# Quarters of a projection moved between transposes and behind score products in a hybrid decoder layer

## The chip, the cores and the metric

The kernel runs on one core of a Trainium2 chip. The metric is the time of one execution on the device in microseconds; several executions are taken and their median is given. The profile is of one further execution. Engines are TensorE (PE in the rows), VectorE (DVE), ScalarE (ACT), GpSimd (POOL) and SyncE (SP), which here only issues transfers.

## The reference, cut to what matters

One decoder layer on 1024 tokens of width 1024, in float32. A combined input projection `u = x @ w_in` is split by columns among four causal mixers and their merge gates; the four results are projected, gated, summed and projected again, and a mixture of 64 experts follows.

```
u = x @ w_in
(conv_in, swa_q, swa_k, swa_v, ret_q, ret_k, ret_v, ret_g,
 nsa_q, nsa_kc, nsa_vc, nsa_ks, nsa_vs, nsa_kw, nsa_vw, nsa_gate, merge_gate) = jnp.split(u, ...)
y_conv = conformer_conv(conv_in, ...) @ p_conv
y_swa = banded_attention(swa_q, swa_k, swa_v, ..., window 128, sink) @ p_swa
y_ret = retention(ret_q, ret_k, ret_v, ret_g, ...) @ p_ret
y_nsa = native_sparse_attention(nsa_q, ...) @ p_nsa
merged = (gts[..., 0, :] * y_conv + gts[..., 1, :] * y_swa
          + gts[..., 2, :] * y_ret + gts[..., 3, :] * y_nsa)
x = layer_norm(ALPHA * x + merged @ w_out)
x = layer_norm(ALPHA * x + moe_ffn(x))
```

## The kernel before, in words

The kernel has two parts, `front` (the mixers) and `back` (output projection, experts). The change is in `front` alone, whose engines all walk one list of items, `SCHEDULE`, written out by the function `schedule`. Each engine takes from every item what is its own, in the order of the list; semaphores tie the engines together. So to move an item in the list moves it on TensorE, ScalarE, VectorE and GpSimd at once.

**The projection.** The columns of `w_in` are cut into 58 chunks of 128. A chunk has two halves of 512 tokens, and a half has two quarters of four of the eight contraction steps: quarter `q` belongs to chunk `q // 4`, half `q // 2 % 2`. A quarter is 12 matmuls of 128x512 (L620), since weights and x are each split into a high and a low part and three products are summed. The halves alternate between PSUM banks 0 and 1. When an odd quarter is done, ScalarE copies the half out (`half`); for the 32 chunks of merge gates this is a tanh into `gate_out` and a store of 256 KB to `gates` (L848, L850), which first waits until the store of two halves ago has landed. After each fourth quarter GpSimd splits the weights of the chunk two ahead (L558, L560), and SyncE then loads another (L469). Quarters are always issued in the order of their numbers, 232 in all; `adv(n)` puts the next n of them into the list, `upto(c)` all up to chunk c.

**Fills.** A `fill` is a group of up to eight transposes on TensorE into bank 6 and one copy out of it by ScalarE (L938, L924). All fills share this bank, and each waits for the copy of the one before:

```
B = bank[6]
if f:
    pe.wait_ge(fill_out, f)
```

There are four fills behind the normalisation of each of two pairs of retention heads (`ret_norm` on VectorE, which ends with `ret_fin`, L1118), two for `swa_v`, one for the gates of the sparse attention, two for `vsvw`, one for `pe`, eight behind the compressed scores, and in both attentions one to four per pair of heads, which carry the probabilities to the products with the values (`pv`, L812).

**Attention.** The function `attention` walks over pairs of heads and blocks. In slot k it issues the score product of pair k+1 (`score`, L790, banks 2 to 5), VectorE's maxima of it (`max`, which end in `m_neg`, L1145 and L1148), VectorE's norms of pair k (L1162, L1166), the fills of pair k-1 with ScalarE's exponentials of pair k+1 behind the last of them, and `rate` quarters, counted by a running debt over the fills. A score product waits for the maxima of all pairs before it (`pe.wait_ge(max_done, 2 * p)`), the fills of a pair for its norms. The sliding-window attention has 16 pairs and two quarters per pair. The sparse attention has 32, alternately `win` (up to 5 key blocks) and `sel` (up to 8), and what quarters are left, divided by 30.

**Order of the parts around the change.** Retention of pair 0, more chunks, retention of pair 1, the `swa_v` fills, sliding-window attention (quarters 121 to 152), fills for gate, vsvw and pe, nine quarters, hidden products of the compression (L745) with a quarter after each, compressed scores with three quarters each, sparse attention (quarters 196 to 231, the last one behind the first fill of its last but one slot).

**Behind the attention.** SyncE waits until all 232 quarters are done (`half_done`), since the loads that follow overwrite their operands: merge weights `p_raw` (L492), then eight pieces of the stored branch results `yt` (L503), the last of them only when the last attention tile is stored, and the gates (L498). ScalarE and VectorE split the pieces into high and low parts (L993, L1226). TensorE multiplies by the merge weights, eight column groups j of two halves (L833), and VectorE gates and sums them (L1237, L1240); from the second group on a half waits for the merge of the half before in the same banks.

Of the kernel before, what the change touches and what calls it, by code (L numbers as in the profile page):

```python
# [163 lines left out]
def schedule():  # L164

    items = [('xt', g) for g in range(8)] + [('mm', 0), ('mm', 1)] + [('xt', g) for g in range(8, 16)]
    state = dict(q=2, fill=0, pv=0)
    last = 4 * NCH  # L170

    def adv(n):
        for _ in range(n):
            if state['q'] < last:
                items.append(('mm', state['q']))
                state['q'] += 1

    def upto(c):
        adv(max(0, 4 * c - state['q']))

    def fill(kind, *a):
        items.append(('fill', state['fill'], kind, a))
        state['fill'] += 1

    upto(WHERE['ret_q', 0])
    items.append(('conv_h',))
    for k in range(CONV_K):
        items.append(('tap', k))
        adv(2 if k % 3 == 0 else 1)
    adv(2)  # L190
    for c in ('conv_mean', 'conv_var', 'conv_out'):
        items.append((c,))
        adv(4)

    def retention(p):
        items.append(('ret_a', p, 0))
        for n in range(NT):
            adv(1)
            if n + 1 < NT:
                items.append(('ret_a', p, n + 1))  # L200
            items.append(('ret_b', p, n))
        items.append(('ret_norm', p))
        adv(11)
        for g in range(4):
            fill('ret', p, g)
        items.append(('ret_store', p))
    upto(WHERE['ret_g', (0, 1)] + 1)
    retention(0)
    upto(WHERE['ret_g', (1, 1)] + 1)
    retention(1)  # L210
    upto(WHERE['swa_v', 0] + 1)
    for g in range(2):
        fill('swa_v', g)
        adv(1)

    def attention(pairs, rate):


        debt = 0.0
        waiting = []  # L220

        def product():

            pr, blocks = waiting.pop()
            items.append(('pv', state['pv'], pr['p'], blocks))
            pr['last_pv'] = state['pv']
            state['pv'] += 1
            if pr['c'] == 1 and pr['kind'] != 'win' and blocks[-1] == pr['nb'] - 1:
                items.append(('out', pr['kind'], pr['n']))

        def both(what, k):
            for e in range(2):
                items.append((what, 2 * pairs[k]['p'] + e))
        for k in range(-1, len(pairs) + 1):
            if k + 1 < len(pairs):
                pr = pairs[k + 1]
                if pr['kind'] == 'sel' and pr['c'] == 0:
                    items.append(('sel_table', pr['n']))
                items.append(('score', pr['p']))
                both('max', k + 1)  # L240
            if 0 <= k < len(pairs):
                both('norm', k)
            if k < 1 and k + 1 < len(pairs):
                both('exp', k + 1)
            if k >= 1:
                prev = pairs[k - 1]
                groups = [tuple(range(a, min(a + 2, prev['nb']))) for a in range(0, prev['nb'], 2)]
                prev['first_fill'] = state['fill']
                prev['last_fill'] = state['fill'] + len(groups) - 1
                for g, blocks in enumerate(groups):  # L250
                    fill('pair', prev['p'], blocks, state['pv'] + len(waiting))
                    if g == len(groups) - 1 and k + 1 < len(pairs):
                        both('exp', k + 1)
                    debt += rate / len(groups)
                    adv(int(debt))
                    debt -= int(debt)
                    if waiting:
                        product()
                    waiting.append((prev, blocks))
        product()  # L260
    attention(SWA, 2.0)
    upto(WHERE['gate', 0] + 1)
    fill('gate')
    for g in range(2):
        fill('vsvw', g)
    fill('pe')
    adv(9)
    for l in range(0, CMP_LEN, HID_STEP):
        items.append(('hidden', l))
        adv(1)  # L270
    items.append(('hidden_t',))
    adv(1)
    items.append(('compress',))
    adv(1)
    for n in range(NT):
        items.append(('cmp_score', n))
        adv(3)
        fill('cmp', n)
    attention(NSA, (last - state['q']) / (len(NSA) - 2))
    adv(last)  # L280
    return items


SCHEDULE = schedule()


# [2005 lines left out]
```

## Time and profile before

| | |
|---|---|
| time, three runs | 2136.57 us median (2134.29 to 2140.7) |
| the profiled execution | 2132.68 us; its span 2130.9 us |
| mean granted clock of TensorE | 0.985 |
| busy share of the span | TensorE 95%, VectorE 63%, ScalarE 40%, GpSimd 26% |
| first score, sliding window / sparse | 422.35 us / 693.92 us |
| last product with the values ends | 932.37 us |

Times in rows are microseconds from the span's start. In a timeline a row is one instruction or a run of equal ones: start, time busy, engine, source line, operation, output and inputs, count; in brackets the idle time of the engine before it and what ended that. The granted clock is a share of full speed (2.4 GHz); its lower level is 0.50 (1.2 GHz). Matmuls overlap in the pipeline, so their starts are compared, not their durations.

### The profile page before, as it was taken

How to read it: one execution, taken by the hardware profiler on the slowest of the kernel's cores; microseconds unless marked ns; L12 is line 12 of the kernel's file. 1: busy time of each engine (PE TensorE's matmuls, PEld its weight loads, DVE VectorE, ACT ScalarE, POOL GpSimd, SP SyncE). 2: the span in 40 equal slices, each digit the busy share in tenths (PEclk: the TensorE clock that was granted, in tenths of full speed). 3: DMA queues.
4: the chain of work that ended last, by engine and by line, in shares of the span. 5: the costliest groups of instructions: out<-in, count | busy, mean ns of one | idle time of the engine just before them, and what ended most of it. 6: DMA issues, size and time to landing. Idle time of an engine off the chain costs nothing.

```text
span 2130.9 us, 33125 instructions
## 1 busy us (share of the span) xinstructions
PE 2032.9 (95%) x9741; PEld 1443.2 (68%) x9742; DVE 1349.5 (63%) x2792; ACT 852.5 (40%) x1433; POOL 554.5 (26%) x358
## 2 busy tenths in 40 slices
PE   6999999899999999989999979999999999999995
PEld 5887777777778666658745537666666666666662
DVE  2594543444026677768646737777777777777756
ACT  2111221234111344440022336666666666666643
POOL 2343231323312211002110033322323333232324
PEclk8999999999999999999999999999999999999998
DMA  5123211222622111057580267899897989899857
GB/s 183 50 55 94 89 50 40 70 55 56 148 75 80 58 50 36 18 179 266 188 332 30 109 268 223 304 347 345 308 352 263 350 300 336 309 303 313 300 172 201
DMA packets 167729, 389.05 MB, mean 183 GB/s; under 512 B 26176, under 2 KB 98145, under 8 KB 142944
## 3 DMA queue, kind: packets, MB, share of 16 engines
q1 hardware_dynamic: 129680, 298.02, 38.4%
q0 software_dynamic: 28752, 73.18, 13.9%
q10 hardware_dynamic: 9216, 16.78, 2.1%
q8 instruction: 49, 0.80, 0.2%
q14 instruction: 32, 0.26, 0.0%
HBM read 337.04 MB, written 80.22 MB: 196 GB/s over the span
## 4 chain that ended last, share of the span: by engine, by line
PE 36%; DMA 8%; issue 3%; DVE 2%; ACT 1%; ACTq 0%; DVEq 0%; POOLq 0%; POOL 0%
PE e_bank L1652 8%; DMA work<-x1d,idx 7%; PE e_bank L1637 7%; PE e_bank L1577 5%; PE e_bank L1615 3%; PE e_bank L1585 3%; PE e_bank L1633 2%; PE e_bank L1634 2%; PE e_bank L1635 2%; ACT d_hi L1921 1%; PE e_bank L1605 1%; PE e_bank L1686 1%; PE e_bank L1723 1%; PE e_bank L1786 1%; PE e_bank L1664 0%
## 5 line engine op out<-in xcount | busy, mean ns | idle before, releaser
L620 PE MATMUL a_bank<-x_hi,w_hi 128*128 128x512 f32 x928 | 375.7, 405 | 9.1 <-DVE x_lo L1016 9.1
L620 PE MATMUL a_bank<-x_hi,w_lo 128*128 128x512 f32 x928 | 365.2, 394 | 0.0
L620 PE MATMUL a_bank<-x_lo,w_hi 128*128 128x512 f32 x928 | 364.8, 393 | 0.0
L1637 PE MATMUL e_bank<-w_gu,work 128*128 x616 | 277.1, 593 | 2.2 <-issue 1.4
L2152 DVE TENSOR_TENSOR d_lo<-w_d,d_hi 128x1024 fp32r<-128x1024 f32 x152 | 179.7, 1224 | 59.9 <-ACT d_hi L1921 59.9
L620 PEld LDWEIGHTS a_bank<-x_hi,w_hi 128*128 128x128 f32 x928 | 176.6, 190 | 50.6 <-issue 13.5
L620 PEld LDWEIGHTS a_bank<-x_hi,w_lo 128*128 128x128 f32 x928 | 176.3, 190 | 38.6
L620 PEld LDWEIGHTS a_bank<-x_lo,w_hi 128*128 128x128 f32 x928 | 176.7, 190 | 34.7 <-issue 0.5
L558 POOL CAST w_hi<-w_raw 128x1024 fp32r<-128x1024 f32 x56 | 65.6, 1171 | 507.8 <-PE a_bank L620 507.8
L1637 PEld LDWEIGHTS e_bank<-w_gu,work 128*128 128x128 f32 x616 | 111.8, 191 | 113.4 <-issue 113.4
L1833 ACT ACTIVATE u_hi<-w_gu 128x1024 fp32r x150 | 159.1, 1061 | 2.0 <-POOL work L1526 1.7
L1921 ACT ACTIVATE d_hi<-w_d 128x1024 fp32r x152 | 152.3, 1049 | 5.6 <-issue 3.6
L560 POOL TENSOR_TENSOR w_lo<-w_raw,w_hi 128x1024 fp32r<-128x1024 f32 x56 | 145.5, 2598 | 4.6
L1541 POOL DMA_INDIRECT acc_odd<-work,idx_out x38 | 86.3, 2271 | 202.9 <-DVE idx_out L2173 189.3
L1541 POOL DMA_INDIRECT acc<-work,idx_out x38 | 80.1, 2108 | 209.6 <-issue 189.7
L1838 ACT ACTIVATE norm<-e_bank 128x256 f32<-128x256 f32 x76 | 29.2, 384 | 252.2 <-PE e_bank L1635 248.4
L1652 PE MATMUL e_bank<-d_hi,h_hi 128*128 128x512 f32 x304 | 126.4, 416 | 0.0
L1496 POOL DMA_INDIRECT work<-x1d,idx x77 | 82.3, 1069 | 166.0 <-DVE idx L2117 143.9
L1633 PE MATMUL e_bank<-u_hi,x_g_hi 128*128 128x512 f32 x300 | 124.7, 416 | 0.0
L1652 PE MATMUL e_bank<-d_hi,h_lo 128*128 128x512 f32 x304 | 120.7, 397 | 0.0
L938 ACT ACTIVATE reg_a<-a_bank 128x512 f32<-128x512 f32 (+2 forms) x106 | 58.5, 552 | 152.4 <-PE a_bank L627 151.0
L1652 PE MATMUL e_bank<-d_lo,h_hi 128*128 128x512 f32 x304 | 119.4, 393 | 0.0
(361 smaller groups left out, 3791.7 us busy)
## 6 DMA issues: line engine op xcount, KB each, us to landing
w_d<-in_moe_wd SPq DMA_DIRECT2D x64, 1024.0 KB, 13.3
w_gu<-in_moe_wg SPq DMA_DIRECT2D x64, 1024.0 KB, 7.7
w_gu<-in_moe_wu SPq DMA_DIRECT2D x64, 1024.0 KB, 11.8
w_raw<-in_w_in SPq DMA_DIRECT2D x54, 512.0 KB, 3.8
gates<-gate_out ACTq DMA_DIRECT2D x64, 256.0 KB, 2.0
g_sb<-gates SPq DMA_DIRECT2D x16, 1024.0 KB, 5.1
acc_odd<-zero POOLq DMA_DIRECT2D x9, 512.0 KB, 14.1
work<-in_w_out SPq DMA_DIRECT2D x4, 1024.0 KB, 8.3
```

The lines of the kernel that those rows point to most:

```text
L558: pool.tensor_copy(w_hi[:, c % 2, :, :], w_raw[:, c % 2, :, :]).then_inc(w_hi_ready, 1)
L560: pool.tensor_tensor(w_lo[:, c % 2, :, :], w_raw[:, c % 2, :, :], w_hi[:, c % 2, :, :].bitcast(F32), ALU.subtract).then_inc(w_lo_ready, 1)
L620: ins = pe.matmul(bank[h][:, :], w[:, c % 2, k, :], x[:, k, cols], start=(k == 0 and j == 0), stop=(k == KD - 1 and j == 2))
L1496: pool.indirect_dma_start(out=x_g[:, s, :], out_offset=None, in_=x1d[:, :], in_offset=bass.IndirectOffsetOnAxis(ap=idx[:, s:s + 1], axis=0 ...
L1541: pool.indirect_dma_start(out=(acc, acc_odd)[s][:, :], out_offset=bass.IndirectOffsetOnAxis(ap=idx_out[:, s:s + 1], axis=0), in_=y_out[:, ...
L1577: ins = pe.matmul(bank[2 * (t % 2) + h][:, :], merged[:, k, t * P:(t + 1) * P], w_out[:, k, h * HALF:(h + 1) * HALF], start=k == 0, stop=k ...
L1633: pe.matmul(out, hi, u_hi[:, j, :, i, :], start=False, stop=False)
L1637: ins = pe.matmul(out, x_gt[:, s, k, :], w_gu[:, bass.ds(e & 3, 1), :, k, :].rearrange('p a m f -> p (a m) f'), start=k == 0, stop=k == KD ...
L1652: ins = pe.matmul(bank[2 + h][:, :], x[:, j, :], w[:, j, cols], start=j == 0 and i == 0, stop=j == 1 and i == 2)
L1833: act.activation(up_part(u_hi[:, j, :, :, :]), up_weights(slot, j), ACT.Copy).then_inc(u_hi_ready, 1)
L1921: act.activation(d_hi[:, j, :], w_d[:, bass.ds(e & 3, 1), j, :].rearrange('p a f -> p (a f)'), ACT.Copy).then_inc(d_hi_ready, 1)
L2152: dve.tensor_tensor(d_lo[:, j, :], w_d[:, bass.ds(slot, 1), j, :].rearrange('p a f -> p (a f)'), d_hi[:, j, :].bitcast(F32), ALU.subtract) ...
```

## The change

Only `schedule` is changed. In the retention two quarters fewer stand between `ret_norm` and the fills, and one stands behind each of the four fills. One is added ahead of the `swa_v` fills. In both attentions one quarter stands behind the score product (and its maxima) in slots -1 and 0. One each is put ahead of the gate fill, of the two vsvw fills and of the pe fill, and three fewer stand behind that one. The rest follows by the running number: the sliding-window attention now has quarters 124 to 157, the hidden products begin behind quarter 167 instead of 161, the compressed scores behind 177 instead of 171, and the sparse attention gets 202 to 231, two behind its first scores and 28 at a rate of 1.0 per pair (before: 36 at 1.2). All other operations, sizes and buffers are the same.

```
@@ -200,15 +200,17 @@
         items.append(('ret_norm', p))
-        adv(11)
+        adv(9)
         for g in range(4):
             fill('ret', p, g)
+            adv(1)
         items.append(('ret_store', p))
...
     upto(WHERE['swa_v', 0] + 1)
+    adv(1)
     for g in range(2):
         fill('swa_v', g)
         adv(1)
@@ -238,6 +240,8 @@
                 items.append(('score', pr['p']))
                 both('max', k + 1)
+            if k < 1:
+                adv(1)
             if 0 <= k < len(pairs):
                 both('norm', k)
@@ -260,11 +264,14 @@
     attention(SWA, 2.0)
     upto(WHERE['gate', 0] + 1)
+    adv(1)
     fill('gate')
     for g in range(2):
+        adv(1)
         fill('vsvw', g)
+    adv(1)
     fill('pe')
-    adv(9)
+    adv(6)
     for l in range(0, CMP_LEN, HID_STEP):
```

## Rows read from the trace of the kernel before

**Rows 1.** The page: busy time, share of the span, instructions.

```profile
PE 2032.9 (95%) x9741; PEld 1443.2 (68%) x9742; DVE 1349.5 (63%) x2792; ACT 852.5 (40%) x1433; POOL 554.5 (26%) x358
```

**Rows 2.** Waits on TensorE, 0 to 1060 us: total, times, longest.

```profile
PE a_bank L627 <- ACT reg_a L938: 5.6, 14, 0.7
...
PE a_bank L790 <- DVE m_neg L1148: 4.0, 2, 2.4
```

**Rows 3.** Timeline of ScalarE in the retention: a half copied out.

```profile
305.00 0.60 ACT L869 ACTIVATE reg_b<-a_bank 128x512 f32<-128x512 f32 x1 [4.84 <-PE a_bank L620]
```

**Rows 4.** Timeline of TensorE at the swa_v fills.

```profile
415.80 0.66 PE L627 MATMUL a_bank<-a_const,reg_a 128*128 128x128 f32 x4 [0.69 <-ACT reg_b L938]
...
419.05 0.60 PE L627 MATMUL a_bank<-a_const,reg_a 128*128 128x128 f32 x4
419.40 0.48 PE L620 MATMUL a_bank<-x_hi,w_hi 128*128 128x512 f32 x1
```

**Rows 5.** Timeline of VectorE: end of the second normalisation.

```profile
399.30 2.29 DVE L1118 TENSOR_TENSOR reg_b<-reg_b 128x2048 f32<-128x2048 f32 x1
```

**Rows 6.** Timeline of TensorE: the first fill of retention pair 1.

```profile
410.49 0.60 PE L627 MATMUL a_bank<-a_const,reg_b 128*128 128x128 f32 x4
```

**Rows 7.** Timeline of TensorE: gate and pe fills, first hidden products.

```profile
543.66 0.66 PE L627 MATMUL a_bank<-a_const,reg_b 12*128 12x12 f32 x8
...
547.35 0.24 PE L627 MATMUL a_bank<-a_const,pe_n 32*128 32x32 f32 x1 [0.69 <-ACT reg_b L938]
...
572.21 1.94 PE L745 MATMUL a_bank<-reg_a,reg_s 64*63 64x256 f32 x16
```

**Rows 8.** Timeline of TensorE: start of the sliding-window attention.

```profile
422.35 0.49 PE L790 MATMUL a_bank<-reg_a 64*128 64x128 f32 x4
...
432.42 0.40 PE L620 MATMUL a_bank<-x_hi,w_hi 128*128 128x512 f32 x1
```

**Rows 9.** Stretches: length; busy PE, PEld, DVE, ACT, POOL; PEclk, DMA share, GB/s.

```profile
425.00:430.00 5.00, 3.13 (x14) 2.01 (x11) 4.39 (x17) 2.74 (x12) 0.00 (x0) 0.55 0.22 65
...
702.00:704.00 2.00, 2.00 (x6) 1.59 (x5) 0.78 (x4) 0.12 (x2) 0.00 (x0) 0.50 0.00 0
...
920.00:930.00 10.00, 9.58 (x82) 6.79 (x82) 3.01 (x7) 5.65 (x11) 0.00 (x0) 1.00 0.51 160
```

**Rows 10.** Timeline of TensorE: start of the sparse attention.

```profile
693.92 0.49 PE L790 MATMUL a_bank<-reg_b 64*128 64x128 f32 x4
...
705.73 0.49 PE L790 MATMUL a_bank<-reg_b 64*128 64x128 f32 x4
```

**Rows 11.** Timeline of VectorE: maxima of the last win and sel pair.

```profile
903.70 0.88 DVE L1140 SCALAR_TENSOR_TENSOR reg_s<-a_const,a_bank 128x512 f32<-128x512 f32 x2 [1.59 <-PE a_bank L790]
...
912.28 1.28 DVE L1140 SCALAR_TENSOR_TENSOR reg_s<-reg_a,a_bank 128x512 f32<-128x512 f32 x2 [2.58 <-PE a_bank L790]
```

**Rows 12.** Timeline of TensorE: last win score, fills, last products.

```profile
902.31 1.35 PE L790 MATMUL a_bank<-reg_b 64*128 64x512 f32 x8
...
919.90 0.66 PE L627 MATMUL a_bank<-a_const,reg_s 128*128 128x128 f32 x4
...
923.84 0.66 PE L627 MATMUL a_bank<-a_const,reg_s 128*128 128x128 f32 x4
...
930.95 1.42 PE L812 MATMUL a_bank<-reg_a,reg_b 128*64 128x128 f32 x16
```

**Rows 13.** Timeline of VectorE behind the attention.

```profile
929.18 0.83 DVE L1214 CAST p_hi<-p_raw 128x1280 fp32r<-128x1280 f32 x1 [5.85 <-DMA p_raw<-in_p_nsa]
...
952.31 2.20 DVE L1240 TENSOR_TENSOR work<-work,term 128x512 f32<-128x512 f32 x1
```

**Rows 14.** Stretch, y_lo (L1226) alone: length, VectorE busy, PEclk, DMA share, GB/s.

```profile
932.00:951.00 19.00, 11.66 (x8) 0.91 1.00 356
```

**Rows 15.** Timeline of SyncE: first load behind the last quarter.

```profile
923.35 0.37 SPq L492 DMA_DIRECT2D p_raw<-in_p_conv  x1
```

**Rows 16.** Timeline of TensorE: second column group of the merge.

```profile
957.55 0.47 PE L833 MATMUL a_bank<-y_hi,p_hi 128*128 128x512 f32 x1 [4.88 <-DVE work L1240]
```

More of the change, by code:

```diff
@@ L202, in retention @@
         items.append(('ret_norm', p))
-        adv(11)
+        adv(9)
         for g in range(4):
             fill('ret', p, g)
+            adv(1)
         items.append(('ret_store', p))
@@ L211, in schedule @@
     upto(WHERE['swa_v', 0] + 1)
+    adv(1)
     for g in range(2):
@@ L240, in attention @@
                 both('max', k + 1)
+            if k < 1:
+                adv(1)
             if 0 <= k < len(pairs):
@@ L262, in schedule @@
     upto(WHERE['gate', 0] + 1)
+    adv(1)
     fill('gate')
     for g in range(2):
+        adv(1)
         fill('vsvw', g)
+    adv(1)
     fill('pe')
-    adv(9)
+    adv(6)
     for l in range(0, CMP_LEN, HID_STEP):
```

## Prediction

> **What bounds the kernel now.** I read the page first. TensorE is busy for 95% of the span [rows 1], so time can come only from its idle gaps, from stretches at the lower clock, or from work that is removed; this change removes none. The list of waits on TensorE for the mixer part (0 to 1060 us) then says what the gaps are [rows 2]: 14 waits of up to 0.7 us for a copy out of bank 6 into `reg_a` alone, and waits of up to 2.4 us of score products for `m_neg`. No projection matmul (L620) waits there after the start-up, so the 58 weight chunks arrive and are split in time. The timelines around the edited places give the prices.
>
> **Unit prices.** A half of a chunk is two quarters, and its copies out start 5.44 us apart (0.60 of work, 4.84 of waiting for TensorE) [rows 3], so a quarter is 2.72 us. Two fills in a row start 1.34 us apart, 0.66 of work and 0.69 of idle [rows 4]. A fill between quarters holds the stream from 419.05 to 419.40, and the next matmul follows 0.09 us late: 0.44 us. So an edge of two fills that gets a quarter saves 1.34 - 0.44 = 0.90 us. The quarter costs nothing extra, being taken from elsewhere, except about 0.09 us at each side where the stream is cut.
>
> **Retention and swa_v fills.** Three edges in each of the two groups, and one between the last retention fill of pair 1 and the first `swa_v` fill, get quarters: 7 x 0.90 = 6.3 us. The first fill comes two quarters (5.44 us) earlier. In pair 1, the tighter one, VectorE's chain of the normalisation ended at 401.59 [rows 5] and the fills began at 410.49 [rows 6]: a margin of 8.9 us, of which 3.5 are left, so this costs nothing; were it gone, the price would be the missing time itself. On GpSimd the splits of two later weight chunks now stand ahead of the `yt` store; both find their chunk's quarters done by the time of the last fill's copy, so the store goes out at about the old time, and ScalarE asks for it only at `nsa_q`, eight quarters (22 us) later. SyncE's loads follow the splits and are as far ahead as before.
>
> **Gate, vsvw and pe fills.** They run from 543.66 to 547.35, 3.69 us up to the last one [rows 7]. Apart, they need about 0.6 + 0.44 + 0.44: 2.2 us saved. ScalarE's queue is passed as well: the copies out of quarters 159 and 161 (each with a gate store) now stand ahead of the copies of vsvw and pe. pe's fill comes after four quarters and three fills, 12.5 us behind the attention's end, and the hidden products six quarters later, at 28.9; now they are at 572.21 - 543.66 = 28.5 [rows 7]. So VectorE's sums for them have some 15 us where they had 24, and the two weight loads that GpSimd starts at the attention's end keep their cover.
>
> **First two score products.** Sliding window: from the first score (422.35) to the matmul at which the old spacing is back (432.42) are 10.07 us [rows 8]. The work in it is two scores of 128 columns (0.42 each), one of 256 (0.63), a fill (0.20) and nine matmuls (2.07): with the seams 3.9. So 6.1 us go: about 3.7 of idle (waits for `m_neg`), the rest because the granted clock was 0.55 of full speed on average behind those gaps, so mostly at its 1.2 GHz level [rows 9]. A quarter (2.72) is longer than the chain it covers (at most 2.4 from score to score), so both scores find their banks free. Sparse attention: 693.92 to 705.73, 11.81 us [rows 10], with three scores, a fill and one quarter in it: 4.3. That is 7.5 us, again with a dip, to 0.50 [rows 9]. Cutting the stream at four new places takes 0.7 us back.
>
> The Trainium skill ("TensorE: Matmul & The Clock Gate", Terms) prices a half-clock stretch at its length times one half; the two dips, some 5.4 and 6.3 us, would be worth 2.7 and 3.2 us, about 1 us more together than the rows give, an estimate from that page that would put the total 1 us lower.
>
> **What the sparse attention loses.** It gets 30 quarters instead of 36: two behind the first scores and then one per pair instead of 1.2, so that they run out after the 28th pair, three slots earlier. The total of quarters is the same, so what is taken here is a saving only if the loop becomes shorter by it. In its slots VectorE mostly waits for the score product, 1.6 and 2.6 us in the last two [rows 11], so TensorE sets the pace and the loop shortens by each quarter taken from a slot that had two. Three costs: the quarter now stands behind a slot's last fill and no longer between two, where it saved 1.34 - (923.84 - 919.90 - 2.72) = 0.12 us [rows 12], some 12 times: 1.5 us. Where a slot's wait of VectorE is shorter than the quarter taken (1.6 against 2.72), a part doesn't come back; the slots that had two quarters have longer waits as a rule, so I allow 0.5 us. The tail, from the last win score: 30.06 us now (902.31 to 932.37) with three quarters in it [rows 12]. Without them the last sel score comes when the win maxima are done (3.7 us from 903.70: 907.4 on the old scale), its own maxima start at 909.7 behind two norms and take 5.3 (twice 1.28, 1.22 and 0.15, the first from [rows 11]), the win norms end at 916.9, seven fills with their products follow (9.9): 926.8. So 5.6 us of 8.2 are gained, 2.6 lost. Together 4.6 us.
>
> **What it gains behind the attention.** SyncE waits for the last quarter (`half_done`), then loads the merge weights and the pieces of `yt`. Now this starts at 923.35, VectorE stands idle 5.85 us until 929.18, and the pieces land late, so that the second column group starts, after a wait of 4.88 us, at 957.55, 25.2 us after the attention's end (932.37) [rows 13, 15, 16]. In the new order the last quarter ends some 25 us ahead of the attention's end, and all but the last piece are in SBUF by then; SyncE no longer stands behind a full queue when the last tile is stored. What is left is the chain of splits: ScalarE's first split ends at +1.5 us, VectorE's seven `y_lo` behind it take 11.66 - 1.22 = 10.4 [rows 14], a VectorE sum beside GpSimd's p_lo took 2.20 us instead of 0.69 [rows 13], so 1.5 more, then the first half's merge of seven operations of 0.72, 5.0; with 0.8 for the seams +19.2. Gain 6 us. Bounds: 0, if the last piece, which can't leave before the last tile's store, still lands at the old distance; 8, if p_lo isn't in VectorE's way.
>
> **Sum.** 6.3 + 2.2 + 6.1 + 7.5 - 0.7 - 4.6 + 6.0 = 22.8 us. The expert part behind has no timer of its own: it starts from the merge, with the same loads, so the gain is carried to the end. The profiled execution took 2132.68 us (span 2130.9), 3.9 us under the median of the three runs shown; 2132.7 - 22.8 = 2109.9, and by the median 2136.6 - 22.8 = 2113.8. I take 2114. A measurement here can't tell less than 0.3%, 6.4 us, from no change.
>
> **Rivals.**
> (a) The merge takes no profit: the last piece or the gates (1 MB each) end last anyway. For it: the last `yt` piece depends on the last tile. Against it: VectorE's 5.85 us of idle are a wait for the first load. Then 16.8 us, 2120; chance 0.13.
> (b) The uncovered tail falls to the lower clock. For it: the clock fell behind gaps of 1.6 to 2.4 us at both attention starts, and the tail will have one of about 2. Against it: between 920 and 930, with one quarter and many small products, it was 1.00 [rows 9]. A dip like the two seen costs 2 to 3 us; with a tail that loses all of its 8.2, 9 us in all: 2123; chance 0.09. The Trainium skill (same page, A second HAM failure mode) says that cycling through PSUM banks with small idle gaps between groups makes the clock swing; that speaks for this rival; the trace of the tail as it is now doesn't agree, with its 1.00.
> (c) No measurable change: the gaps close, but the same time comes back as VectorE-bound slots through the whole sparse loop (6 quarters, 16.3 us, not given back). Against it: VectorE's waits in [rows 11]. 2136.6 - 22.8 + 16.3 = 2130, at the edge of what can be told; chance 0.04.
> (d) Slower: one quarter per pair is too little work to hold the clock in the sparse loop. Each microsecond at the lower level costs half of one, so from 46 us of the loop's 238 on the gain is gone, and from 58 on it is measurably slower; at half of the loop, 119 us, 59.5 - 22.8 is 37 us slower, 2173. Against it: the same stretch of 920 to 930, with 12 quarter matmuls in 10 us, which is less than one quarter per pair gives, had 1.00 [rows 9]. Chance 0.03.
> (e) More than forecast: the tail loses nothing and the merge gains 8: 22.8 + 2.6 + 2 = 27 us or more, 2109 and below; chance 0.08.
> The forecast, 19 to 27 us (2110 to 2118), has 0.63. The range 2104 to 2124 takes in (a), (b) and most of (e) and leaves out (c) and (d). Faster: 0.63 + 0.13 + 0.09 + 0.08 = 0.93, less 0.01 for a (b) that runs deeper; same 0.05; slower 0.03.
>
> **What the new profile would show.** No wait of 0.69 us before transposes on `reg_a` or `reg_b` in the retention, swa_v and vsvw fills, and none on `m_neg` at the second and third score; clock 1.00 at both attention starts; the fills at the old margin less 5.4 us behind `ret_fin`; the merge weights' load more than 20 us ahead of the last product; a gap of about 2 us in the last slots; second column group some 19 us behind the attention's end. The prediction is wrong if the gaps are closed and the sparse loop has kept its length, or if the clock dips move into the tail.

## The result

The changed kernel takes 2109.66 us (median of 4 executions, 2107.53 to 2110.41), the kernel before in the same session 2136.94 us (median of 4, 2134.29 to 2140.7). The ratio is 0.9866, with a 95% interval from 0.9855 to 0.9878: 27.3 us faster by the medians. The profiled execution took 2109.28 us with a span of 2107.5 us and a mean granted clock of 0.988 of full speed (before: 2132.68, 2130.9 and 0.985), 23.4 us less. The forecast was 2114, a sum of 22.8 us. Executions more than 1.5% above the fastest one of their kernel, eight in all, are left out of every median of this document.

Line numbers in `front` are seven higher in the changed kernel: transposes L634, quarters L627, scores L797, products L819, merge L840.

Waits on TensorE of the changed kernel from 0 to 1060 us (total, times, longest) answer to [rows 2]:

```profile
PE a_bank L634 <- ACT reg_a L945: 5.1, 16, 0.3
...
PE a_bank L840 <- DVE y_lo L1233: 2.4, 2, 1.2
PE a_bank L634 <- DVE reg_s L1173: 2.2, 2, 1.9
PE a_bank L840 <- DVE work L1247: 1.7, 1, 1.7
```

Of the waits for `reg_a`, the longest is now 0.3 us where it was 0.7; the waits of score products for `m_neg` are gone. So are these, of the fills of retention pair 1, of `swa_v` and of `pe`, which the kernel before had too:

```profile
PE a_bank L627 <- ACT reg_b L938: 4.1, 6, 0.7
```

The longest wait for `reg_s` is now 1.9 us, where it was 1.2: the uncovered tail. VectorE's last operation of the second normalisation answers to [rows 5]:

```profile
397.10 2.29 DVE L1125 TENSOR_TENSOR reg_b<-reg_b 128x2048 f32<-128x2048 f32 x1
```

It ends at 399.39. The timeline of TensorE at the fills of the second retention pair, at the `swa_v` fills and at the first sliding-window score answers to [rows 6, 4, 8]:

```profile
402.85 0.60 PE L634 MATMUL a_bank<-a_const,reg_b 128*128 128x128 f32 x4
...
406.06 0.60 PE L634 MATMUL a_bank<-a_const,reg_b 128*128 128x128 f32 x4
...
418.37 0.60 PE L634 MATMUL a_bank<-a_const,reg_a 128*128 128x128 f32 x4
...
424.86 0.49 PE L797 MATMUL a_bank<-reg_a 64*128 64x128 f32 x4
```

A fill and a quarter take 3.21 us together, with no wait in brackets, and the first fill has 3.5 us of margin behind 399.39, as reckoned. The last sliding-window product, the gate fill and the pe fill stand for [rows 7]:

```profile
544.77 1.09 PE L819 MATMUL a_bank<-reg_a 128*64 128x128 f32 x16
...
548.74 0.67 PE L634 MATMUL a_bank<-a_const,reg_b 12*128 12x12 f32 x8
...
558.69 0.24 PE L634 MATMUL a_bank<-a_const,pe_n 32*128 32x32 f32 x1
```

The `pe` fill comes 12.8 us behind the attention's end (545.86), where 12.5 were reckoned.

The first, second and fourth score of the sparse attention, two regular scores, the last two scores, the last fill with a wait and the last product stand for [rows 10, 12]:

```profile
696.90 0.49 PE L797 MATMUL a_bank<-reg_b 64*128 64x128 f32 x4
...
700.26 0.49 PE L797 MATMUL a_bank<-reg_b 64*128 64x128 f32 x4
...
707.18 0.49 PE L797 MATMUL a_bank<-reg_b 64*128 64x128 f32 x4
...
862.94 1.45 PE L797 MATMUL a_bank<-reg_b 64*128 64x512 f32 x6
...
872.38 1.13 PE L797 MATMUL a_bank<-reg_b 64*128 64x512 f32 x4
...
889.94 1.35 PE L797 MATMUL a_bank<-reg_b 64*128 64x512 f32 x8
...
895.17 1.99 PE L797 MATMUL a_bank<-reg_b 64*128 64x512 f32 x8
...
904.59 0.63 PE L634 MATMUL a_bank<-a_const,reg_s 128*128 128x128 f32 x4 [1.86 <-DVE reg_s L1173]
...
913.01 1.42 PE L819 MATMUL a_bank<-reg_a,reg_b 128*64 128x128 f32 x16
```

The three stretches whose clock was in question answer to [rows 9] (columns as there; PEclk is the third number from the right):

```profile
425.00:430.00 5.00, 5.00 (x26) 3.77 (x27) 2.61 (x11) 1.92 (x7) 3.42 (x2) 1.00 0.18 59
700.00:710.00 10.00, 9.15 (x48) 6.72 (x47) 7.90 (x32) 3.46 (x14) 3.44 (x2) 1.00 0.19 55
900.00:910.00 10.00, 7.52 (x74) 5.03 (x73) 9.06 (x19) 5.71 (x11) 0.00 (x0) 1.00 1.01 350
```

Behind the attention, SyncE's first load answers to [rows 15], VectorE's cast, one of its `y_lo` groups and its slowed sum to [rows 13, 14]:

```profile
889.45 0.37 SPq L499 DMA_DIRECT2D p_raw<-in_p_conv  x1
```

```profile
906.57 0.82 DVE L1221 CAST p_hi<-p_raw 128x1280 fp32r<-128x1280 f32 x1
...
917.75 9.03 DVE L1233 TENSOR_TENSOR y_lo<-work,y_hi 128x2048 fp32r<-128x2048 f32 x6 [0.57 <-ACT y_hi L1000]
...
928.13 2.04 DVE L1247 TENSOR_TENSOR work<-work,term 128x512 f32<-128x512 f32 x1
```

The merge's second column group started 18.8 us behind the attention's end at 914.43 (913.01 + 1.42), and the last product of the merge 115.6 us behind that end:

```profile
933.22 0.47 PE L840 MATMUL a_bank<-y_hi,p_hi 128*128 128x512 f32 x1 [1.67 <-DVE work L1247]
...
1029.98 0.39 PE L840 MATMUL a_bank<-y_hi,p_lo 128*128 128x512 f32 x1
```

In the trace of before the same row, the last product of the merge, is 123.5 us behind 932.37:

```profile
1055.86 0.39 PE L833 MATMUL a_bank<-y_hi,p_lo 128*128 128x512 f32 x1
```

**Where the time came from.** Quarters are the same work in another place, so between two points of the list the gain is the time before, less the time after, plus 2.72 us for each quarter that the new order has more ahead of the second point. These quarters are counted in the list: 3 ahead of the first sliding-window score, 5 by the last sliding-window product, 6 by the first sparse score, 3 by the last win score, none by the end.

| up to | before | after | gain so far | this part | forecast |
|---|---|---|---|---|---|
| first sliding-window score | 422.35 | 424.86 | 5.65 | fills 5.7 | 6.3 |
| last sliding-window product | 542.64 | 544.77 | 11.5 | first scores 5.8 | 6.1 |
| first sparse score | 693.92 | 696.90 | 13.3 | gate, vsvw, pe 1.9 | 2.2 |
| last win score | 902.31 | 889.94 | 20.5 | first sparse scores and loop 7.2 | 4.8 |
| end of the attention | 932.37 | 914.43 | 17.9 | tail -2.6 | -2.6 |
| last merge product | 1055.86 | 1029.98 | 25.9 | merge 7.9 | 6.0 |

The 4.8 are 7.5 for the scores, less 0.7 of seams and 2.0 for the loop. The first row also holds a difference that the change did not make: the same copy out of the projection, ahead of all edits, starts 0.36 us later in the changed kernel.

```profile
283.24 0.60 ACT L869 ACTIVATE reg_b<-a_bank 128x512 f32<-128x512 f32 x1 [2.90 <-PE a_bank L620]
```

```profile
283.60 0.60 ACT L876 ACTIVATE reg_b<-a_bank 128x512 f32<-128x512 f32 x1 [2.90 <-PE a_bank L627]
```

Counted from this copy, the fills gave 8.16 - (141.26 - 139.11) = 6.0 us.

From the last merge product to the last instruction the changed kernel took 1077.5 us and the kernel before 1075.0, so 2.5 us are not carried to the end of this pair of profiles, and 23.4 are left. The instructions there are the same in every kernel of this document, and their fourteen profiles have 1075.0 to 1080.4 us for them; the kernel before has the shortest.

### The profile page after: what moved, and what is told of

Read it like the earlier page. It is cut to its first block and busy times, and to the rows that moved or that the text cites. A ratio compares the mean times of both kernels' runs of the same rounds, so it can differ in the third digit from the quotient of the medians.

```text
span 2107.5 us, 33125 instructions
## 1 busy us (share of the span) xinstructions
PE 2027.0 (96%) x9741; PEld 1438.3 (68%) x9742; DVE 1338.0 (63%) x2792; ACT 851.8 (40%) x1433; POOL 552.3 (26%) x358
## 5 line engine op out<-in xcount | busy, mean ns | idle before, releaser
L627 PE MATMUL a_bank<-x_hi,w_hi 128*128 128x512 f32 x928 | 374.9, 404 | 8.9 <-DVE x_lo L1023 8.9
L627 PE MATMUL a_bank<-x_hi,w_lo 128*128 128x512 f32 x928 | 364.1, 392 | 0.0
L627 PE MATMUL a_bank<-x_lo,w_hi 128*128 128x512 f32 x928 | 363.4, 392 | 0.0
L627 PEld LDWEIGHTS a_bank<-x_hi,w_hi 128*128 128x128 f32 x928 | 175.5, 189 | 50.6 <-issue 13.5
L627 PEld LDWEIGHTS a_bank<-x_hi,w_lo 128*128 128x128 f32 x928 | 175.3, 189 | 38.3
L627 PEld LDWEIGHTS a_bank<-x_lo,w_hi 128*128 128x128 f32 x928 | 175.8, 189 | 34.3 <-issue 0.5
L855 ACT ACTIVATE gate_out<-a_bank 128x512 f32<-128x512 f32 x64 | 38.2, 598 | 204.7 <-PE a_bank L627 204.6
## 6 DMA issues: line engine op xcount, KB each, us to landing
w_d<-in_moe_wd SPq DMA_DIRECT2D x64, 1024.0 KB, 12.8
w_gu<-in_moe_wu SPq DMA_DIRECT2D x64, 1024.0 KB, 11.3
```

What stands on the lines that cost most here:

```text
L627: ins = pe.matmul(bank[h][:, :], w[:, c % 2, k, :], x[:, k, cols], start=(k == 0 and j == 0), stop=(k == KD - 1 and j == 2))
```

## Experiments

All were timed in five rounds against the kernel before, on one chip per set. "Difference" is the median less the median of before in the same set (2138.77, 2138.42 and 2139.05 us).

| kernel | median us | ratio, 95% interval | difference |
|---|---|---|---|
| e1_ret | 2129.94 | 0.9957, 0.9942 to 0.9971 | -8.8 |
| e2_gate | 2131.99 | 0.9967, 0.9954 to 0.9979 | -6.8 |
| e3_swa | 2130.61 | 0.9957, 0.9941 to 0.9973 | -8.2 |
| e4_nsa | 2126.24 | 0.9935, 0.9921 to 0.9949 | -12.5 |
| e5_cover | 2120.45 | 0.9919, 0.9906 to 0.9932 | -18.0 |
| e6_early | 2115.15 | 0.9884, 0.9868 to 0.9900 | -23.3 |
| e7_warm | 2135.40 | 0.9989, 0.9979 to 0.9998 | -3.0 |
| e8_after | 2112.12 | 0.9881, 0.9867 to 0.9896 | -26.3 |
| e9_tail | 2113.56 | 0.9874, 0.9859 to 0.9889 | -25.5 |
| e10_mid | 2115.98 | 0.9885, 0.9869 to 0.9901 | -23.1 |
| e11_after | 2110.53 | 0.9868, 0.9853 to 0.9883 | -28.5 |
| e0_before | 2138.18 | 0.9997, 0.9988 to 1.0006 | -0.9 |

### One part at a time

The kernel before with one part of the change each. The retention part:

```diff
-        adv(11)
+        adv(9)
         for g in range(4):
             fill('ret', p, g)
+            adv(1)
...
     upto(WHERE['swa_v', 0] + 1)
+    adv(1)
```

> Only the retention and swa_v fills get their quarters; the sparse attention then has 33 quarters at 1.1 per pair and keeps them to its end. Theory (each part returns its own idle time, and nothing else moves): 6.3 us less than before for seven edges of 0.90 us, 5.5 to 6.5 in the profile from the end of the fills on. Rival (time closed here opens again in the attention, which has fewer quarters): under 2 us.

The gate, vsvw and pe part:

```diff
+    adv(1)
     fill('gate')
     for g in range(2):
+        adv(1)
         fill('vsvw', g)
+    adv(1)
     fill('pe')
-    adv(9)
+    adv(6)
```

> Only the gate, vsvw and pe fills get their quarters (one quarter more stands there in all). Theory: 2 us less, which the time alone can hardly tell and the profile can: hidden products some 0.8 us later than before with one quarter more done. Rival (ScalarE's gate stores ahead of the copies delay the pe fill): a wait of TensorE at the hidden products, 0 or slower.

The two score parts, each with the other attention left out:

```diff
+            if k < 1 and pairs is SWA:
+                adv(1)
```

> Only the first two scores of the sliding-window attention get a quarter each. Theory: 6 us less, 3.7 of idle and 2.3 from the clock, which stays at 1.00 there. Rival (the clock falls anyway, later): 3.7 us. The sparse attention keeps its quarters to the end, so the merge gains nothing.

```diff
+            if k < 1 and pairs is NSA:
+                adv(1)
```

> Only the first two scores of the sparse attention get a quarter each; its other 34 quarters go at 1.2 per pair, so they run out about two slots before the last one. Theory: 7 us at the start, about 2 lost in the tail, 5 to 6 gained at the merge, because the loads start earlier: 10 to 11 us less. Rival (the merge gains nothing from earlier loads): 5 us less.

By the medians each part alone gained 2 to 5 us more than expected, and the four differences sum to 36.3 us where the whole gives 26 to 28.5. Each part's own stretch doesn't have that surplus. Between two points, with the quarters counted:

- retention: three quarters more ahead of the first sliding-window score, 8.16 - (424.40 - 422.35) = 6.1 us (6.0 from the copy at 283.24)
- gate, vsvw, pe: from the last sliding-window product to the first sparse score 152.14 us with one quarter more, where it was 151.28: 2.72 - 0.86 = 1.9 us
- sliding-window scores: from the first score to the last product 119.89 us with two quarters more, where it was 120.29: 5.8 us
- sparse scores: from the first sparse score (696.11) to the last merge product (1045.99) 349.88 us, with the same quarters in between, where it was 361.94: 12.1 us

The sum is 25.9, that of the whole in the table above. But this leaves out what each edit does outside its own stretch. The next table has all of them, as differences from the profile of before, with the quarters counted and the fills measured from the copy at 283.24. "Between" is from the last sliding-window product to the first sparse score, "sparse" from there to the attention's end, "merge" from there to its last product.

| kernel | fills | sliding window | between | sparse | merge | together |
|---|---|---|---|---|---|---|
| e1_ret | -6.0 | 0.1 | 1.2 | -1.6 | 1.0 | -5.3 |
| e2_gate | 3.0 | -0.5 | -1.9 | -4.0 | 1.1 | -2.3 |
| e3_swa | 2.9 | -5.8 | 1.4 | -3.7 | 0.9 | -4.3 |
| e4_nsa | 2.8 | 0.1 | 0.0 | -4.1 | -8.0 | -9.2 |
| changed | -6.0 | -5.8 | -1.9 | -4.6 | -7.9 | -26.2 |

Two things stand out. The sparse attention of e1_ret, e2_gate and e3_swa is 1.6 to 4.0 us shorter, though nothing was edited in it: it has 33 to 35 quarters in place of 36, at another rate. Of this, 0.9 to 1.4 us lie between its first and fourth score; what the rest is was not tested. This gain stands in three of the parts, and the whole can have it once at most.

And the fills took 2.8 to 3.0 us longer in three kernels that have them as before; in e7_warm, below, it was 2.9. The waits there are the same as in [rows 4], but behind them the clock fell, in e2_gate for instance, where four transposes took 1.11 us in place of 0.66:

```profile
416.41 1.11 PE L630 MATMUL a_bank<-a_const,reg_a 128*128 128x128 f32 x4 [0.69 <-ACT reg_b L941]
```

```profile
415.00:420.00 5.00, 4.24 (x15) 3.44 (x16) 0.00 (x0) 1.21 (x3) 0.72 (x1) 0.66 0.43 170
```

The two profiles of the kernel before don't have this fall, and the eight profiles of kernels with the new fills don't either: from the copy to the first sliding-window score they agree to 0.1 us. e0_before, below, comes back to it.

Waits of e4_nsa on TensorE from 690 to 1060 us show that this part alone brings the merge's gain, since it alone of the four makes the quarters end early:

```profile
PE a_bank L835 <- DVE y_lo L1228: 2.4, 2, 1.2
...
PE a_bank L835 <- DVE work L1242: 1.7, 1, 1.7
```

In e1_ret the same wait for `work` is still the 4.9 us of [rows 16]:

```profile
951.20 0.77 PE L835 MATMUL a_bank<-y_hi,p_hi 128*128 128x512 f32 x1 [4.85 <-DVE work L1242]
```

### The clock alone

The kernel before with the idle gaps filled by matmuls whose results nobody reads (this adds work and moves no quarter):

```diff
+KEEP = (6, 6, 5, 8)
...
                     ins.then_inc(score_done, 1)
+                    if p in (0, 1, len(SWA), len(SWA) + 1):
+                        spare, done = (1, 60) if p < 2 else (0, 97)
+                        pe.wait_ge(half_out, done)
+                        for k in range(KEEP[p % 2 + 2 * (p > 1)]):
+                            pe.matmul(bank[spare][:, :], x_hi[:, k % KD, HALF:HALF + P], x_hi[:, k % KD, 0:HALF], start=True,
+                                      stop=True)
```

> The kernel before, with the idle gaps behind the first two score products of both attentions filled with matmuls whose results nobody reads (25 of 128 columns of weights by 512, into a free bank); no quarter is moved. It tells the clock's share of the 6 and 7 us of the score products apart from that of the idle time. If the granted clock fell because of those gaps, it is 1.00 at 430 and 705 us and the kernel is 2.4 us (first attention) and 2.6 to 3 us (second) faster, together about 5 us, with a gap as long as before. If the gaps weren't the reason, the two dips stay and the time is that of before, or longer by what the filling runs over.

The stretch of [rows 9] behind the first sliding-window scores and one behind the first sparse scores, in e7_warm:

```profile
425.00:430.00 5.00, 3.98 (x21) 2.55 (x21) 4.02 (x18) 2.81 (x13) 0.00 (x0) 1.00 0.36 98
701.00:705.00 4.00, 4.00 (x21) 3.03 (x21) 2.66 (x14) 1.38 (x5) 0.00 (x0) 1.00 0.01 4
```

The clock stays at full speed where it was 0.55 and 0.50. From the first score to the last product the sliding-window attention takes 118.41 us (423.11 to 541.52) and took 120.29, 1.9 less; from the first sparse score to the start of the last product are 234.67 us (692.79 to 927.46) and were 237.03, 2.4 less. Together 4.2 us, less whatever the filling itself costs, and 3.0 by the medians (ratio 0.9979 to 0.9998, 0.4 to 4.5 us). So the gaps did cause the two falls of the clock, and a third of what the quarters gain there is the clock. The other profiles agree: the five with the gaps at the first sparse scores open (both of before, e1_ret, e2_gate, e3_swa) have 0.50 to 0.58 from 700 to 705 us, all others 1.00.

### The tail against the merge

The changed kernel with the sparse attention's quarters spread otherwise:

```diff
-    attention(NSA, (last - state['q']) / (len(NSA) - 2))
+    attention(NSA, (last - state['q'] - 2) / (len(NSA) - 2))
```

> The changed kernel with one edit: the quarters left for the sparse attention are spread over all of its slots, as before the change, so that the last slots have quarters in them again. If the two terms of my sum stand (the uncovered tail costs 2.6 us, the early end of the quarters gives the merge 6.4 us), the attention ends some 2.6 us earlier than in the changed kernel, SyncE's load for the merge starts only some 10 us ahead of its end, the second column group starts 25 us behind it instead of 18.8, and the whole is about 3 to 4 us slower than the changed kernel (ratio 1.0015 to 1.002). Rival: the merge takes no profit from the early end, and this is 2 to 3 us faster.

with `(last - state['q'] - 2) / (len(NSA) - 7)`:

> The changed kernel with one edit: the quarters of the sparse attention run out some five slots earlier than in the changed kernel. If the merge's gain is already complete with the changed kernel's 25 us of lead (what is left is the chain of splits behind the last tile), the second column group stays at 18.8 us behind the attention's end, and five more slots have no cover: where VectorE sets their pace, each loses up to the 2.7 us of its quarter, so 5 to 10 us slower than the changed kernel. Rival: the longer lead gives the merge more, or the slots without quarters shorten by the whole quarter: equal time. A third: with some 20 us of small products alone the granted clock falls, and then it is slower by several us more.

and with `(last - state['q'] - 1) / (len(NSA) - 2)`:

> The changed kernel with one edit between the two spreadings of the quarters seen so far: the last quarter comes some 17 us ahead of the attention's end, where the changed kernel has 25 and the kernel with quarters to the end 10.5. The load for the merge, the split and the sums need some 15 us. If so, the merge keeps its 115.8 us (it took 123.1 with 10.5 us of lead) and the later slots are covered better: equal to the changed kernel or up to 2 us faster. Rival: each microsecond of lead under 25 is paid in the merge, and it is 3 to 4 us slower.

The merge's part of the expectations for e5_cover and e6_early held. In e5_cover SyncE's first load went out at 906.08, 10.3 us ahead of the attention's end, and both waits are back:

```profile
PE a_bank L840 <- DVE work L1247: 4.9, 1, 4.9
PE a_bank L840 <- DVE y_lo L1233: 4.2, 3, 1.7
...
PE a_bank L634 <- DVE reg_a L1173: 2.8, 2, 2.2
PE a_bank L797 <- DVE m_neg L1155: 2.7, 2, 1.4
```

Its merge ended 122.9 us behind the attention (1039.24 - 916.38), e6_early's 115.7 with some 50 us of lead, e10_mid's 115.8 with 25. e4_nsa's ended 115.5 us behind with 23.7. So the gain is complete at 24 to 25 us of lead and gone at 10.

The attention's part was not as expected. e5_cover spread 28 quarters over 30 slots, and so its third slot has none. The timeline of TensorE there:

```profile
701.82 0.49 PE L797 MATMUL a_bank<-reg_b 64*128 64x128 f32 x4
...
703.93 0.49 PE L797 MATMUL a_bank<-reg_b 64*128 64x128 f32 x4 [1.25 <-DVE m_neg L1155]
...
706.65 0.45 PE L634 MATMUL a_bank<-a_const,reg_s 128*128 128x128 f32 x1 [2.22 <-DVE reg_a L1173]
```

and its clock just behind (in the changed kernel 1.00, above):

```profile
705.00:710.00 5.00, 3.35 (x9) 2.80 (x10) 3.86 (x16) 1.14 (x5) 0.78 (x1) 0.57 0.40 105
```

From the third to the fifth score are 11.3 us; the changed kernel takes 8.7 with a quarter more in them. One missing quarter costs 5.3 us there, more than the 2.6 of the tail that e5_cover wanted back: 8.3 us slower than e8_after of the same set, where 3 to 4 were expected. e10_mid has the same hole, is 5.5 us slower than e11_after of its set where the expectations had 2 us faster or 3 to 4 slower, and has 25 us of lead (with its tail at the lower clock) instead of the 17 that I had reckoned, so it doesn't show where between 10 and 25 us the merge starts to pay.

e6_early is 3.0 us slower than e8_after, where 5 to 10 were expected: of its last five slots, two (from the scores at 869.76 and 876.48) took 6.7 and 5.7 us where they take 9.4 and 7.9, so they gave back most of the quarter of 2.72 us.

### The clock in the tail

e8_after and e11_after are the changed kernel itself:

> The changed kernel itself once more, on the same chip as the three others of this set, so that differences of 3 us can be read. Expected 27 us (ratio 0.987) below the kernel before.

> The changed kernel once more, as the reference of this set on the same chip: 27 us (ratio 0.987 to 0.988) below the kernel before, with or without the fall of the clock in the tail.

From the copy at 283.24 to the last sel score their profiles and the first one of the changed kernel agree to 0.2 us; behind it they differ in two places, in the tail and in the merge. The last sel score, the wait and the last product of e8_after:

```profile
893.61 1.99 PE L797 MATMUL a_bank<-reg_b 64*128 64x512 f32 x8
...
903.02 0.63 PE L634 MATMUL a_bank<-a_const,reg_s 128*128 128x128 f32 x4 [1.86 <-DVE reg_s L1173]
...
915.08 1.42 PE L819 MATMUL a_bank<-reg_a,reg_b 128*64 128x128 f32 x16
```

The wait is the same 1.86 us, but from the score to the end are 22.9 us instead of 19.3, and the clock behind the wait is at its lower level:

```profile
905.00:910.00 5.00, 5.00 (x31) 3.02 (x31) 2.32 (x3) 1.08 (x3) 0.00 (x0) 0.50 0.72 211
910.00:915.00 5.00, 4.94 (x32) 3.29 (x30) 1.92 (x2) 1.70 (x3) 0.00 (x0) 0.58 0.00 0
```

In e11_after it was 1.00 from 900 to 920, as in the first profile of the changed kernel; in e9_tail, e6_early, e10_mid and e4_nsa it fell as in e8_after, the last three behind waits of 2.0 to 2.2 us.

The second place is the merge. In e11_after the clock fell behind the wait for `work`, which was 0.3 us longer than in the first profile:

```profile
932.79 0.47 PE L840 MATMUL a_bank<-y_hi,p_hi 128*128 128x512 f32 x1 [1.95 <-DVE work L1247]
```

```profile
930.00:935.00 5.00, 3.05 (x11) 2.14 (x10) 4.79 (x8) 0.00 (x0) 0.00 (x0) 0.84 0.15 40
```

From here to the last merge product e11_after took 98.3 us, e9_tail (wait of 2.0 us) too, as the kernel before (98.3); the profiles with waits of 1.7 to 1.8 us, the first one and e8_after among them, took 96.8. So e8_after lost 3.6 us in the tail and e11_after 1.5 in the merge; with the differences at the start and in the expert part their spans came out alike, 2109.4 and 2109.3 us.

e9_tail was to fill the gap in the tail:

```diff
+KEEP = 2
...
+                        if p == len(PAIRS) - 1 and blocks[0] == 0:
+                            pe.wait_ge(half_out, 2 * NCH)
+                            for k in range(KEEP):
+                                pe.matmul(bank[0][:, :], vsvw[:, k, :], vsvw[:, 4:8, :], start=True,
+                                          stop=True)
```

> The changed kernel with its one gap in the tail filled: ahead of the first fill of the last sel pair, where TensorE waits 1.86 us for VectorE, two matmuls of 128 columns of weights by 512 go into a free bank and nobody reads them. If that gap is what lets the granted clock fall in the tail in some executions (two profiles of the changed kernel have the same waits, but 17.6 and 21.2 us from the last sel score to the last product, with a clock of 1.00 and of 0.50 to 0.58), the profile has 1.00 there, the attention ends 17.6 us behind its last sel score, and the median is 1 to 3 us below that of the changed kernel; its highest execution comes down too. If the clock falls for another reason, there is no difference, or 0.3 us more for the filling.

It missed its place. The gap stands ahead of the fill of the last pair but one, and the two matmuls came some 6 us behind it:

```profile
903.49 0.63 PE L635 MATMUL a_bank<-a_const,reg_s 128*128 128x128 f32 x4 [1.86 <-DVE reg_s L1179]
...
909.19 3.00 PE L744 MATMUL a_bank<-reg_b 128*128 128x512 f32 x4
```

So it only added work behind a clock that had fallen already: 24.0 us from the last sel score to the end, where e8_after took 22.9. Its median is 3.0 us above e11_after, and its four executions (2110.45 to 2116.24 us) overlap with that one's (2109.65 to 2113.88). Whether a filled gap keeps the clock in the tail stays open; e7_warm shows it for the two attention starts alone.

### The kernel before once more

> The kernel before once more, for a second profile of it. The single parts took 9, 7, 9 and 14 us off its median, 39 together, where the whole takes off 27 to 28, and its first profiled execution (2132.7 us) is below all but one of its 17 timed ones. If that execution was a lucky one, this one shows where its usual 2136 to 2140 us come from: I expect more stretches at the lower clock behind the gaps of the retention's fills (near 309 and 415 us, where three of the single parts have them) and a longer part behind the merge (1077 to 1080 us where it was 1075). The rival is that the single parts share a gain that the whole has only once; then this profile looks like the first one.

The profile looks like the first one, so my expectation failed: the last merge product is at 1055.85 (it was 1055.86), the clock at 309 and 415 us did not fall, and the part behind the merge took 1076.8 us. The rival said that the single parts share a gain that the whole has only once, and the table of the parts bears it out in part: the sparse attention.

But this profiled execution, at 2134.43 us, was again the fastest of its kernel's eleven. Over the 51 executions of before in these sets, whose median is 2138.7 us, the mean granted clock and the time go together: on average 2137.0 us at 0.985 (6 executions), 2138.4 at 0.983 (13), 2141.0 at 0.981 (8). The two with a trace had 0.985 and 0.984. So the usual execution is 4 to 6 us above the traced ones. The likely cause is the clock at the old fills: four of the six profiles of kernels with these fills lose 2.8 to 3.0 us there, and the three of them that keep the gaps of before at one attention start or both (e2_gate, e3_swa, e4_nsa) have a mean clock of 0.983. That is not shown for the kernel before itself, since neither of its traced executions has it. As an estimate it fits: the four parts without that loss are 29.8 us together, and 32.7 if the usual execution of before has it and e1_ret doesn't, against 36.3 by the medians. The changed kernel's three profiles are 26.2, 22.7 and 24.3 us ahead of before's at the end of the merge, counted from the copy at 283.24; their mean and 2.9 are 27.3, which is what the medians say. The expert part, 1075.0 and 1076.8 us in before and up to 1080.4 elsewhere, may hold the rest.

## Why the prediction was right

**Fills.** 6.0 us of 6.3 from the copy at 283.24 on, in the changed kernel and in e1_ret, and the gate part 1.9 of 2.2. The waits of 0.69 us went, at 3.21 us for a fill and a quarter. The margin behind the second normalisation held: no fill waits at 402.85. What the sum lacks is the clock: in executions where it falls behind the old fills, as in e2_gate, the same edit is worth some 9 us.

**First scores.** 5.8 us of 6.1 for the sliding window; for the sparse attention, from its first to its fourth score, 11.81 - 10.28 and two quarters, 7.0 of 7.5. The split into idle and clock is shown by e7_warm: 4.2 us of clock in all, where the rows gave 2.4 for the first attention and about as much for the second. The Trainium skill ("TensorE: Matmul & The Clock Gate", Terms) prices the two falls, at the lengths that the prediction gave them, at 2.7 and 3.2 us, 5.9 together; the measured 1.9 and 2.4 are below it, and so the measurement decides. The prediction had these falls too short, besides: in the trace of before the clock is at 0.50 from 425.5 to 432.0 us and from 698.5 to 705.0, 6.5 us each and not 5.4 and 6.3.

**The loop.** This cost is the step that was too high. I took off 1.5 us for the quarter's new place and 0.5 for slots bound by VectorE; neither is seen, and from the fourth sparse score to the last win score 0.2 us were gained. The slot from the score at 862.94, with one quarter now, takes 872.38 - 862.94 = 9.4 us; with two it took 12.0, in the kernel before:

```profile
872.93 1.77 PE L790 MATMUL a_bank<-reg_b 64*128 64x512 f32 x8
...
884.93 1.35 PE L790 MATMUL a_bank<-reg_b 64*128 64x512 f32 x8
```

The slot from 889.94, with none now, takes 5.2 and took 7.9 with one. Both give back about the whole 2.7 us.

**The tail.** 2.6 us lost, as worked out, in two of three profiles of the changed kernel. In the third, rival (b) happened: 3.6 us more, on the same waits. I had it at 0.09 and priced the fall of the clock at 2 to 3 us. That it is in the spread of the timed executions (2107.5 to 2114.2 us over the three sets) is likely, but not shown. The prediction named this as a sign of being wrong, clock dips that move into the tail: by that sign it was right in the first profile and wrong in e8_after. The Trainium skill (same page, "A second HAM failure mode: psum-queue depth-cycling") speaks of a clock that swings when there are small idle gaps between matmul groups; e8_after agrees with it, with 0.50 at 905 to 910 us, and the stretch of before on which I leaned against it had no such gap.

**The merge.** 7.9 us of 6.0, mis-sized. The second column group came 18.8 us behind the attention's end (19.2 forecast, 25.2 before), which is 6.4; the other 1.5 lie behind it, where the granted clock was 0.79 from 955 to 960 us, behind the wait of 4.88, and is now 1.00 from 930 to 945. These 1.5 us are not certain: e11_after has a fall there and 6.1 us of gain. Rival (a), no profit for the merge, falls with e5_cover.

**The sum.** The terms give 25.9 us at the merge's end where 22.8 were forecast: +2.4 loop and scores, +1.9 merge, -1.2 fills and first scores. So the mechanism was right and two sizes were off in the same direction. That the profiled pair differs by 23.4, close to 22.8, is luck: 2.5 us went in the expert part, which the change doesn't touch. The median moved by 27.3, a little beyond the forecast of 19 to 27 and within the range; the likely rest is the clock at the old fills, which no term has.

## What to carry to other kernels

Price a moved piece of work at both ends: what it covers in its new place, and what waits in the old one. Here the early end of the filler work opened a load behind it, and this gave 6 to 8 us for 2.6 us of uncovered tail, or for 6.2 us of it where the clock fell there. A spreading rate just below one filler per slot left a hole where the slots are short, and one hole cost 5.3 us. Measure each part of a change over the whole stretch that it can reach, and not over its own lines alone: three parts here also shortened a loop that they didn't edit. And where a gap between small matmuls is closed, count the clock behind it, about a third of the gain at the scores here, but read its price from a run that fills the gap and moves nothing.

## What the runs showed of the hardware

The same program with the same waits kept TensorE's full clock through a gap of 1.86 us in two profiled executions and lost it in a third, at a price of 3.6 us in that stretch; so a gap of this size decides nothing alone, and one clean profile doesn't exclude a fall. The fills of before say the same with waits of 0.69 us, one behind each group of four transposes: full clock in two profiles, a fall in four, for 2.8 to 3.0 us. Smaller steps count too: a slot without its quarter, with waits of 1.25 and 2.2 us, was enough for 0.57 at 705 to 710 us in e5_cover.
